# Normalised rows of the expert stage: made on chip from the residual rows, or read from a copy in DRAM

## The chip, the cores and the metric

The kernel runs on one core of a Trainium2 chip. The metric is the device time of one execution in microseconds (us); of several executions the median is given. TensorE (PE) multiplies, VectorE (DVE) and ScalarE (ACT) work on rows, GpSimd (POOL) issues the gathers by index, SyncE (SP) issues all other transfers, and 16 DMA engines carry them out. Each engine takes its instructions in order and waits on semaphores.

## The reference

One layer of a decoder for 1024 prompt tokens and 64 sample tokens (8 sequences of 8, each with 4096 cached positions). What this case is about is the end of the layer:

```
h = x + einsum('btd,de->bte', mixed, w_out)
y = h + peer(rmsnorm(h, norm2_w))
def rmsnorm(x, w):  y = x * rsqrt(mean(x*x, axis=-1) + 1e-6);  return y * w
def peer(xn):       # 8 heads; 128 x 128 product keys
    q = xn @ peer_w_q;  s = q . peer_keys            # two halves of 128 scores a head
    expert = the 16 best pairs of each head;  gate = softmax of their scores
    a = gelu(xn . peer_u[expert])                    # 128 experts a token
    return sum over experts of gate * a * peer_v[expert]
```

Ahead of it stand a projection with pooling mixer and multi-head latent attention (causal over the prompt, paged over the cache for the samples) and a merge with sigmoid gates. Everything is float32; D = 1024. The normalised rows xn are needed twice: transposed for the queries, and row by row for the dots with peer_u.

## The kernel before, in words

Tokens come in nine tiles: eight of 128 prompt tokens and one of 64 sample tokens. The dense work up to the expert scores (class Prompt) is done in three groups of 2, 3 and 3 tiles. Group 0 runs alone; then the expert stage (class Experts) begins and the rest is woven into it: groups 1 and 2, the paged attention of the samples (class Pages), and the dense work of the sample tile (class Sample).

The weaving is by slots. Each engine has a program of the expert stage that yields after each slot (`SLOTS` = 1088 + 20), and `Main.to(slot)` runs that program up to a slot before the dense work emits its next instruction. So the order on every engine is fixed in the code; the slot of a dense piece comes from the class Plan, with planned microseconds.

A slot k belongs to one gather of peer_u and one of peer_v: GpSimd gathers 128 rows of 4 KB by index into a ring of eight buffers (`gather`, L1559), VectorE multiplies them with the normalised rows and sums (`dot`, L1667), after 16 dots come the gelu and a matrix of diagonals, and TensorE multiplies these with the peer_v rows, 20 slots (`LAG`) later (L1622). The buffer of a dot is free for the next gather when the dot is done; that of a peer_v row when its matmuls are.

One gather serves 32 tokens with four heads each, one expert per head, so a dot needs the same 32 normalised rows in each quarter of the 128 partitions: `xrep[j]` holds rows 32j to 32j+31 of the tile four times. There are five such buffers. Their path before the change:

- In the dense part of each group ScalarE squares and sums a row of h (L1152) and takes the root (L1154); VectorE inverts it and multiplies row, inverse and norm weight into `xn2` (L1366, L1368). TensorE transposes `xn2` for the queries (L952).
- SP stores h to `h_dram` (L624) and `xn2` to `xn2_dram` (L626; the trace writes xn_dram). The norm weight, repeated over 128 partitions (512 KB), is loaded in each group (L615) and for the samples (L2172).
- For tile 0 SP loads the four `xrep` buffers with 16 transfers (L637). For each later tile SP loads the rows from `xn2_dram` into one buffer `xt` at slot 80 of the tile before (L1588), and ScalarE copies them into `xrep[j]` in `replicate`, four copies of 32 rows for each j (L1636), 24, 12, 8 and 4 slots before the tile begins; the copies wait until the old content of the buffer has been used.
- The residual rows are loaded from `h_dram` at slot 60 of their tile (L1593), VectorE adds the experts' sum to them (`collect`, L1708), and SP stores the output (L1604).

SP's order around the first group: rows are stored as they come (`keep_rows`), the first three query weights are loaded (`load_peer`, L640), SP waits for the stores, issues the 16 loads, then the loads of the next group (`begin`), then the fourth query weight and the scores' stores (`keep_scores`).

Of the kernel before, what the change touches and what calls it, by code (L numbers as in the profile page):

```python
# [8 lines left out]
ALU = mybir.AluOpType  # L9
# [5 lines left out]
P = 128  # L15
# [64 lines left out]
def build(nc, I, O):  # L80
    with ExitStack() as ctx:
# [7 lines left out]
        for name, shape in (("new_rows", [NS, KL + DR]), ("s_dram", [ROUTES, P, 2 * NK]), ("h_dram", [TOK, D]), ("xn2_dram", [TOK, D]),  # L89
# [197 lines left out]
class Prompt:  # L287
# [145 lines left out]
    def norm2(self):  # L433
        return self.buf(18496, D)

# [43 lines left out]
    def begin(self, main, g):  # L479
# [7 lines left out]
        else:  # L487
            sp.wait_ge(self.rows_stored, 32 * g.tile0)
# [8 lines left out]
        if g.first:  # L497
# [3 lines left out]
            sp.dma_start(self.wukT[0:DN], I["w_ukT"]).then_inc(self.ukT_in, 16)  # L501

# [86 lines left out]
    def load_merge(self, main, g):  # L589
# [25 lines left out]
        sp.dma_start(self.norm2(), I["norm2"]).then_inc(self.res_in, 16)  # L615

    def keep_rows(self, main, g):
        env = self.env
        for t in range(g.tiles):
# [5 lines left out]
            sp.wait_ge(self.xn2_done, tile + 1)  # L625
            sp.dma_start(env["xn2_dram"][dst, :], self.xn2(t)).then_inc(self.rows_stored, 16)  # L626
# [6 lines left out]
        sp.wait_ge(self.rows_stored, 32 * (g.tile0 + g.tiles))  # L633
# [513 lines left out]
    def act_out(self, main, g):  # L1147
        s, ps, st = self.nc.scalar, self.ps, self.stats()
        for q in range(g.tiles):
# [4 lines left out]
            s.activation(st[:, 12 + q:13 + q], st[:, 8 + q:9 + q], ACT.Sqrt, bias=self.C["eps"], scale=1.0 / D).then_inc(self.root2_done, 1)  # L1154
# [198 lines left out]
    def dve_out(self, main, g):  # L1353
        v, ps, st = self.nc.vector, self.ps, self.stats()
        for q in range(g.tiles):
            dve, tile = main.to(g.after("out7", q)), g.tile0 + q
            dve.wait_ge(self.h_done, tile + 1)
            if q == 0:
                dve.wait_ge(self.res_in, 16 * (g.tile0 + g.tiles + g.i + 1))
            y = self.x_row(q)  # L1360
            v.tensor_tensor(y, y, ps[:, 2 + 2 * q:4 + 2 * q, :].rearrange("p a b -> p (a b)"), ALU.add).then_inc(self.h_out, 1)
        for q in range(g.tiles):
            dve, tile = main.to(g.at(f"tp{q}")), g.tile0 + q
            dve.wait_ge(self.root2_done, tile + 1)
            r = st[:, 12 + q:13 + q]
            v.reciprocal(r, r)  # L1366
            v.drain()
            v.scalar_tensor_tensor(out=self.xn2(q), in0=self.x_row(q), scalar=r, in1=self.norm2(), op0=ALU.mult, op1=ALU.mult).then_inc(self.xn2_done, 1)  # L1368

    def dve_scores(self, main, g):  # L1370
        v, ps, i = self.nc.vector, self.ps, g.i
        for j in range(2 * H):
# [5 lines left out]
            if j == 0:  # L1378
                dve.wait_ge(self.rows_stored, 32 * (g.tile0 + g.tiles))
# [120 lines left out]
class Experts:  # L1500
# [4 lines left out]
    def __init__(self, env, sem, ps, rt):  # L1505
# [13 lines left out]
        self.xt = take(D)  # L1519
# [5 lines left out]
        self.a, self.a2, self.th, self.wt = take(2, 16), take(16), take(16), take(16)  # L1525
# [4 lines left out]
        self.x0_in, self.xt_in, self.x_set, self.h_in = sem("i_x0_in"), sem("i_xt_in"), sem("i_x_set"), [sem(f"i_h_in{b}") for b in range(2)]  # L1530
# [873 lines left out]
```

## Time and profile before

| | |
|---|---|
| three timed runs | 3970.24, 3991.52, 3993.34 us, median 3991.52 |
| the profiled execution | 3977.99 us, of which the span of the trace is 3976.2 us |
| busy of the span | PE 3064.3 us (77%), DVE 2684.1 (68%), POOL 2394.3 (60%), ACT 957.7 (24%) |
| transferred | 1387.34 MB, 349 GB/s over the span |
| mean granted clock of TensorE | 0.864 of full speed |

The 40 slices of the page show the DMA engines busy 0.4 to 0.5 of the time up to about 400 us, which is group 0, and 0.8 or more in every slice after that, while VectorE's share goes from 0.5 to 0.8 and back. Such shares are means over stages of different kind; what a stage waits for has to be read from the waits inside it. A wait is put down to what came last. DMA share and GB/s belong together: the share is the mean over 16 engines.

### The profile page before, as it was taken

The page shows a single profiled execution, that of the slowest core. Times are in us where ns is not written, and L with a number is a line of the kernel's source. Part 1 is how long each engine was busy: PE and PEld are TensorE (multiplying, and loading weights), DVE is VectorE, ACT ScalarE, POOL GpSimd, SP SyncE. Part 2 cuts the span into 40 slices and gives each one's busy share as a digit, 9 for nine tenths or more (in the row PEclk, how much of TensorE's full clock was granted, in tenths as well). Part 3 has the DMA queues.
Part 4 walks back from the last instruction along what each step waited for, and adds up shares of the span by engine and source line. Part 5 has one row for each costly group of instructions (what it writes and reads, how often), then busy time and mean ns, then how long its engine had stood idle before and what let it go on. Part 6 is the DMA issues. An engine that isn't in the chain of part 4 may idle for free.

```text
span 3976.2 us, 44748 instructions
## 1 busy us (share of the span) xinstructions
PE 3064.3 (77%) x13299; PEld 1596.3 (40%) x13299; DVE 2684.1 (68%) x6876; ACT 957.7 (24%) x1893; POOL 2394.3 (60%) x2196
## 2 busy tenths in 40 slices
PE   8896888996787888876688888888888866663345
PEld 5665435443442544333344444444444434230001
DVE  2312987665578866666788888888878875656653
ACT  2200123111023320120245444443454411100000
POOL 0000565765676566675766676676667676677776
PEclk9798988997998889998899999899989976666668
DMA  4445798999999989999999999899989999999999
GB/s 132 101 154 186 265 372 326 412 408 373 379 401 388 339 338 411 403 402 373 376 370 331 360 376 358 319 386 362 369 331 365 363 402 414 379 397 383 379 396 376
DMA packets 432834, 1387.34 MB, mean 349 GB/s; under 512 B 60553, under 2 KB 118890, under 8 KB 428306
## 3 DMA queue, kind: packets, MB, share of 16 engines
q0 software_dynamic: 313344, 1140.99, 74.5%
q1 hardware_dynamic: 119250, 243.49, 17.4%
q8 instruction: 109, 1.79, 0.2%
q14 instruction: 131, 1.07, 0.1%
HBM read 1354.17 MB, written 30.11 MB: 348 GB/s over the span
## 4 chain that ended last, share of the span: by engine, by line
PE 31%; DVE 20%; POOL 16%; DMA 15%; issue 10%; DVEq 3%; ACT 3%; SPq 1%; ACTq 0%; POOLq 0%
POOL arena L1559 16%; DMA arena<-in_peer_v,arena 8%; PE ps L1622 6%; DVE arena L1667 6%; PE ps L1872 6%; DMA arena<-in_w_peer 3%; PE ps L713 2%; PE ps L979 2%; DMA arena<-in_peer_u,arena 2%; PE ps L922 2%; DVE arena L2026 2%; PE ps L944 2%; PE ps L1903 2%; PE ps L879 1%; PE ps L856 1%
## 5 line engine op out<-in xcount | busy, mean ns | idle before, releaser
L1667 DVE CUSTOM_DVE_ANT_0 arena<-arena 128x1024 f32<-128x1024 f32 x1088 | 1319.7, 1223 | 562.2 <-DMA arena<-in_peer_u,arena 534.8
L1559 POOL DMA_INDIRECT arena<-in_peer_v,arena x1088 | 1194.0, 1097 | 798.2 <-PE ps L1622 503.6
L1559 POOL DMA_INDIRECT arena<-in_peer_u,arena x1088 | 1198.8, 1102 | 756.3 <-DVEq L1497 385.8
L1622 PE MATMUL ps<-arena 128*32 128x512 f32 x4352 | 693.6, 726 | 446.7 <-DMA arena<-in_peer_v,arena 441.4
L1872 PE MATMUL ps<-arena 128*128 128x512 f32 x1056 | 537.8, 633 | 11.0 <-ACT arena L1965 7.4
L1622 PEld LDWEIGHTS ps<-arena 128*32 128x32 f32 x4352 | 145.4, 124 | 852.3 <-issue 846.1
L979 PE MATMUL ps<-arena 128*128 128x384 f32 (+1 forms) x768 | 248.3, 477 | 57.9 <-DMA arena<-in_w_peer 57.6
L1965 ACT ACTIVATE arena<-ps 128x512 f32<-128x512 f32 x264 | 157.9, 598 | 431.6 <-PE ps L1872 430.0
L1872 PEld LDWEIGHTS ps<-arena 128*128 128x128 f32 x1056 | 188.5, 199 | 172.1 <-issue 162.6
L922 PE MATMUL ps<-arena 128*128 128x384 f32 (+1 forms) x768 | 233.0, 459 | 1.4 <-ACT arena L1135 1.4
L2026 DVE TENSOR_REDUCE arena<-arena 128x8 f32<-128x512 f32 x264 | 180.5, 684 | 79.1 <-ACT arena L1965 66.9
L1880 PEld LDWEIGHTS ps<-arena 128*128 128x128 f32 x1056 | 165.1, 197 | 136.7 <-issue 134.8
L1903 PE MATMUL ps<-arena 128*64 128x257 f32 x528 | 153.9, 443 | 81.5 <-ACT arena L1985 81.4
L979 PEld LDWEIGHTS ps<-arena 128*128 128x128 f32 x768 | 150.1, 202 | 144.6 <-issue 78.9
L713 PE MATMUL ps<-arena 128*128 128x384 f32 (+1 forms) x528 | 170.9, 483 | 21.3 <-DVE arena L1207 21.3
L922 PEld LDWEIGHTS ps<-arena 128*128 128x128 f32 x768 | 146.7, 193 | 91.1 <-issue 20.1
L1952 ACT ACTIVATE arena<-ps 128x256 f32<-128x256 f32 (+1 forms) x264 | 107.7, 408 | 277.3 <-PE ps L1858 154.4
L1880 PE MATMUL ps<-arena 128*128 128x64 f32 x1056 | 150.5, 266 | 0.0
L1636 ACT ACTIVATE arena<-arena 32x1024 f32<-32x1024 f32 x120 | 126.4, 1053 | 92.0 <-DVE arena L1667 90.7
L713 PEld LDWEIGHTS ps<-arena 128*128 128x128 f32 x528 | 102.4, 196 | 91.2 <-issue 34.9
L1903 PEld LDWEIGHTS ps<-arena 128*64 128x64 f32 x528 | 76.3, 155 | 138.9 <-ACT arena L1985 93.4
L1858 PE MATMUL ps<-const,arena 128*128 128x128 f32 x528 | 112.8, 296 | 21.4 <-ACTq L1955 12.6
(232 smaller groups left out, 3719.0 us busy)
## 6 DMA issues: line engine op xcount, KB each, us to landing
arena<-in_w_merge SPq DMA_DIRECT2D x32, 1536.0 KB, 9.3
arena<-in_w_peer SPq DMA_DIRECT2D x64, 576.0 KB, 7.0
arena<-in_cache SPq DMA_DIRECT2D x256, 144.0 KB
arena<-in_peer_u,arena POOLq DMA_INDIRECT x1088, 8.2
arena<-in_peer_v,arena POOLq DMA_INDIRECT x1088, 8.2
arena<-in_w_front SPq DMA_DIRECT2D x33, 512.0 KB, 6.7
arena<-in_w_out SPq DMA_DIRECT2D x24, 512.0 KB, 8.8
arena<-s_dram SPq DMA_DIRECT2D x68, 128.0 KB
```

The lines of the kernel that those rows point to most:

```text
L713: last = t.matmul(bank, w[:, k, :], xnT[:, k, :], start=k == 0, stop=k == KD - 1)
L922: last = t.matmul(ps[:, 2 + 2 * (d % 2) + a, 0:T], ring[:, a * KD + k, :], xnT[:, k, 0:T], start=k == 0, stop=k == KD - 1)
L979: last = t.matmul(ps[:, 2 + j % 2, 0:T], self.p_ring(j % 3)[:, k, :], xn2T[:, k, :], start=k == 0, stop=k == KD - 1)
L1559: self.nc.gpsimd.indirect_dma_start(out=ring[:, slot, :], out_offset=None, in_=self.I[table], in_offset=bass.IndirectOffsetOnAxis(ap=self. ...
L1622: mm = self.nc.tensor.matmul(self.acc[32 * j:32 * j + 32, n, :], self.diag[:, (q0 + j) // 16 % DIAGS, (q0 + j) % 16, :], self.v_ring[:, (q ...
L1636: last = self.nc.scalar.activation(self.xrep[jg % self.XBUF][32 * i:32 * i + 32, :], self.xt[32 * j:32 * j + 32, :], ACT.Copy)
L1667: self.nc.vector.tensor_tensor_reduce(out=u, in0=u, in1=self.xrep[jg % self.XBUF], scale=1.0, scalar=0.0, op0=ALU.mult, op1=ALU.add, accum ...
L1872: last = t.matmul(self.key, self.cTp[:, j % 2, k * P:(k + 1) * P], self.wuk[:, k, :], start=k == 0, stop=k == 1)
L1880: last = t.matmul(out, self.cTp[:, j % 2, k * P:(k + 1) * P], self.qlat[:, k, b * NS:b * NS + NS], start=j + k == 0, stop=False)
L1903: last = self.nc.tensor.matmul(self.acc_ps[0:NS, 0:KL + 1], self.scs[gi % 2][:, j, :], self.source(j, par)[:, 0:KL + 1], start=j == 0, sto ...
L1965: self.nc.scalar.activation(self.sqp[:, j % 2, :], self.key, ACT.Square).then_inc(self.ksq_done, 1)
L2026: self.nc.vector.tensor_reduce(out=self.ssn[:, j, :], in_=self.sqp[:, j % 2, :].rearrange("p (h d) -> p h d", h=H), axis=AX, op=ALU.add).t ...
```

## The change

The array `xn2_dram` goes, with its stores and loads. The inverses of the roots of all nine tiles are kept on chip (`rinv`, one column a tile), and the repeated norm weight is loaded once, at the beginning, into a buffer `w2` that takes the place of `xt`. For tile 0 the 16 transfers read the `xn2` buffer on chip in place of DRAM, and SP waits for their landing before it begins the loads of the next group. For each later tile SP loads the residual rows at slot 80 of the tile before (those of tile 0 at slot 0) into one of the two buffers `h`, from which the output is also formed; VectorE makes 32 normalised rows in the first quarter of `xrep[j]` in `normalise`, at the slots of the old copies, and ScalarE copies them into the other three quarters. The stages before the experts use `w2` and `rinv` too.

```
@@ class Prompt: begin, keep_rows
-            sp.wait_ge(self.rows_stored, 32 * g.tile0)
+            sp.wait_ge(self.rows_stored, 16 * g.tile0)
+            if g.i == 1:
+                sp.wait_ge(self.ex.x0_in, 256)
...
             sp.dma_start(self.wukT[0:DN], I["w_ukT"]).then_inc(self.ukT_in, 16)
+            sp.dma_start(self.ex.w2, I["norm2"]).then_inc(self.ex.w2_in, 16)
...
-        sp.dma_start(self.norm2(), I["norm2"]).then_inc(self.res_in, 16)
...
             sp.dma_start(env["h_dram"][dst, :], self.x_row(t)).then_inc(self.rows_stored, 16)
-            sp.wait_ge(self.xn2_done, tile + 1)
-            sp.dma_start(env["xn2_dram"][dst, :], self.xn2(t)).then_inc(self.rows_stored, 16)
...
         if g.first:
+            sp.wait_ge(self.xn2_done, 1)
             for j in range(4):
                 for i in range(4):
-                    sp.dma_start(self.ex.xrep[j][32 * i:32 * i + 32, :], env["xn2_dram"][32 * j:32 * j + 32, :]).then_inc(self.ex.x0_in, 16)
+                    sp.dma_start(self.ex.xrep[j][32 * i:32 * i + 32, :], self.xn2(0)[32 * j:32 * j + 32, :]).then_inc(self.ex.x0_in, 16)
@@ class Experts: sync
+            if k == 0:
+                self.load_rows(sp, 0)
             t, r = divmod(k, 128)
             if r == 80 and t < PT:
-                rows = P if t + 1 < PT else NS
-                need(sp, self.x_set, 4 * t)
-                sp.dma_start(self.xt[0:rows], self.env["xn2_dram"][(t + 1) * P:(t + 1) * P + rows, :]).then_inc(self.xt_in, 16)
+                self.load_rows(sp, t + 1)
             t, r = divmod(k - LAG, 128)
-            if 0 <= t <= PT and r == 40:
-                rows = P if t < PT else NS
-                need(sp, self.stored[t % 2], 16 * (t // 2))
-                sp.dma_start(self.h[t % 2][0:rows, :], self.env["h_dram"][t * P:t * P + rows, :]).then_inc(self.h_in[t % 2], 16)
...
+    def load_rows(self, sp, t):
+        rows = P if t < PT else NS
+        need(sp, self.stored[t % 2], 16 * (t // 2))
+        sp.dma_start(self.h[t % 2][0:rows, :], self.env["h_dram"][t * P:t * P + rows, :]).then_inc(self.h_in[t % 2], 16)
@@ class Experts: replicate (ScalarE), normalise (VectorE)
         t, j = divmod(jg, 4)
-        act.wait_ge(self.xt_in, 16 * t)
-        if jg >= self.XBUF:
-            t0, j0 = divmod(jg - self.XBUF, 4)
-            act.wait_ge(self.u_used, 128 * t0 + 112 + 4 * j0 + 4)
-        for i in range(4):
-            last = self.nc.scalar.activation(self.xrep[jg % self.XBUF][32 * i:32 * i + 32, :], self.xt[32 * j:32 * j + 32, :], ACT.Copy)
+        act.wait_ge(self.x_one, jg - 3)
+        x = self.xrep[jg % self.XBUF]
+        for i in range(1, 4):
+            last = self.nc.scalar.activation(x[32 * i:32 * i + 32, :], x[0:32, :], ACT.Copy)
         last.then_inc(self.x_set, 1)
...
+    def normalise(self, dve, jg):
+
+        t, j = divmod(jg, 4)
+        dve.wait_ge(self.h_in[t % 2], 16 * (t // 2 + 1))
+        rows = slice(32 * j, 32 * j + 32)
+        self.nc.vector.drain()
+        self.nc.vector.scalar_tensor_tensor(out=self.xrep[jg % self.XBUF][0:32, :], in0=self.h[t % 2][rows, :], scalar=self.rinv[rows, t:t + 1],
+                                            in1=self.w2[rows, :], op0=ALU.mult, op1=ALU.mult).then_inc(self.x_one, 1)
@@ class Experts: vector, at the end of a slot
+            t = (k + 24) // 128
+            if 1 <= t <= PT:
+                for j, ahead in enumerate((24, 12, 8, 4)):
+                    if k == 128 * t - ahead and j < (4 if t < PT else 2):
+                        self.normalise(dve, 4 * t + j)
```

The class Sample loses its own load of the norm weight and its store of normalised rows in the same way, and the counts of `rows_stored` are halved everywhere.

## Rows read from the trace of the kernel before

**Rows 1.** The dots of the expert stage: ns min/median/max, first and last start.

```profile
L1667 DVE CUSTOM_DVE_ANT_0 arena<-arena x1088: 1206/1224/1294, 416.1 to 3942.9; 128x1024 f32<-128x1024 f32 x182
```

**Rows 2.** Windows: busy us of PE, PEld, DVE, ACT, POOL; clock; DMA; GB/s.

```profile
416.00:1960.00 1544.00, 1255.99 (x5193) 635.23 (x5194) 1068.01 (x2626) 282.58 (x532) 994.58 (x912) 0.89 0.98 376
1960.00:3161.00 1201.00, 1040.61 (x4772) 527.35 (x4772) 1018.88 (x2732) 538.52 (x1043) 811.67 (x736) 0.93 0.96 357
3161.00:3976.00 815.00, 429.49 (x2062) 185.91 (x2060) 480.92 (x1171) 69.84 (x147) 580.27 (x538) 0.71 1.00 391
```

**Rows 3.** Waits, 416 to 1960 us: who waited for whom, us, times, longest.

```profile
DVE arena L1667 <- DMA arena<-in_peer_u,arena: 273.5, 149, 10.5
```

**Rows 4.** Waits of VectorE, 1960 to 3161 us.

```profile
DVE arena L2026 <- ACT arena L1965: 58.9, 52, 3.1
DVE arena L2041 <- ACT arena L1976: 25.8, 16, 3.9
```

**Rows 5.** Waits, 3161 to 3976 us.

```profile
DVE arena L1667 <- DMA arena<-in_peer_u,arena: 261.3, 173, 7.8
```

**Rows 6.** DMA issues, 416 to 1960 us: count, KB each, median us to landing.

```profile
xn_dram<-arena SPq DMA_DIRECT2D x6, 512.0 KB
...
arena<-h_dram SPq DMA_DIRECT2D x4, 512.0 KB, 11.1
...
arena<-xn_dram SPq DMA_DIRECT2D x3, 512.0 KB, 11.5
...
arena<-in_norm SPq DMA_DIRECT2D x2, 512.0 KB, 15.3
```

**Rows 7.** DMA issues, 3161 to 3976 us.

```profile
arena<-h_dram SPq DMA_DIRECT2D x2, 512.0 KB, 9.7
...
arena<-xn_dram SPq DMA_DIRECT2D x1, 512.0 KB, 22.1
...
arena<-in_norm SPq DMA_DIRECT2D x1, 512.0 KB, 9.1
...
xn_dram<-arena SPq DMA_DIRECT2D x1, 256.0 KB
arena<-xn_dram SPq DMA_DIRECT2D x1, 256.0 KB, 8.8
arena<-h_dram SPq DMA_DIRECT2D x1, 256.0 KB, 8.5
```

**Rows 8.** The normalisation of 128 rows in the dense part.

```profile
L1368 DVE SCALAR_TENSOR_TENSOR arena<-arena x8: 1284/1285/1286, 284.2 to 1711.9; 128x1024 f32<-128x1024 f32 x8
```

**Rows 9.** ScalarE's copies, 1960 to 3161 us; no wait stands below them.

```profile
L1636 ACT ACTIVATE arena<-arena x48: 1039/1053/1057, 2058.9 to 2971.4; 32x1024 f32<-32x1024 f32 x48
```

**Rows 10.** Timeline of ScalarE at one site of the copies: start us, us.

```profile
2478.30 4.24 ACT L1636 ACTIVATE arena<-arena 32x1024 f32<-32x1024 f32 x4
```

**Rows 11.** Timeline of VectorE for tile 5's sites, with idle time before.

```profile
2479.87 0.28 DVE L1442 MATCH_REPLACE8 arena<-arena 128x128 f32<-128x128 f32 x1
...
2484.88 0.35 DVE L2041 RECIPROCAL arena<-arena 128x32 f32<-128x32 f32 x1 [3.34 <-ACT arena L1976]
...
2555.97 0.69 DVE L2026 TENSOR_REDUCE arena<-arena 128x8 f32<-128x512 f32 x1 [2.52 <-ACT arena L1965]
```

**Rows 12.** Landing of the normalised rows' loads (L1588).

```profile
DMA to landing us min/median/max: 7.7/10.4/22.1
```

**Rows 13.** The gathers of peer_u on GpSimd: ns min/median/max.

```profile
L1559 POOL DMA_INDIRECT arena<-in_peer_u,arena x1088: 932/938/2455, 369.4 to 3932.4; - x182
```

**Rows 14.** The 16 loads of tile 0, and their landing.

```profile
L637 SPq DMA_DIRECT2D arena<-xn_dram x16: 318/421/427, 295.7 to 302.5; - x16
...
DMA to landing us min/median/max: 2.7/3.7/5.9
```

**Rows 15.** Timeline of SP, 303 to 309 us.

```profile
306.34 1.23 SPq L640 DMA_DIRECT2D arena<-in_w_peer  x2
```

**Rows 16.** Timeline of TensorE, 285 to 330 us.

```profile
318.80 6.55 PE L979 MATMUL ps<-arena 128*128 128x256 f32 x16 [12.78 <-DMA arena<-in_w_peer]
```

More of the change, by code:

```diff
@@ L431, in xn2 @@
         return self.buf(15424 + D * t, D)
-    def norm2(self):
-        return self.buf(18496, D)
     def xn2T(self, g):
@@ L1153, in act_out @@
             s.drain()
-            s.activation(st[:, 12 + q:13 + q], st[:, 8 + q:9 + q], ACT.Sqrt, bias=self.C["eps"], scale=1.0 / D).then_inc(self.root2_done, 1)
+            s.activation(self.ex.rinv[:, tile:tile + 1], st[:, 8 + q:9 + q], ACT.Sqrt, bias=self.C["eps"], scale=1.0 / D).then_inc(self.root2_done, 1)
         for q in range(g.tiles):
@@ L1358, in dve_out @@
             if q == 0:
-                dve.wait_ge(self.res_in, 16 * (g.tile0 + g.tiles + g.i + 1))
+                dve.wait_ge(self.res_in, 16 * (g.tile0 + g.tiles))
+                if g.first:
+                    dve.wait_ge(self.ex.w2_in, 16)
             y = self.x_row(q)
@@ L1364, in dve_out @@
             dve.wait_ge(self.root2_done, tile + 1)
-            r = st[:, 12 + q:13 + q]
+            r = self.ex.rinv[:, tile:tile + 1]
             v.reciprocal(r, r)
             v.drain()
-            v.scalar_tensor_tensor(out=self.xn2(q), in0=self.x_row(q), scalar=r, in1=self.norm2(), op0=ALU.mult, op1=ALU.mult).then_inc(self.xn2_done, 1)
+            v.scalar_tensor_tensor(out=self.xn2(q), in0=self.x_row(q), scalar=r, in1=self.ex.w2, op0=ALU.mult, op1=ALU.mult).then_inc(self.xn2_done, 1)
     def dve_scores(self, main, g):
@@ L1378, in dve_scores @@
             if j == 0:
-                dve.wait_ge(self.rows_stored, 32 * (g.tile0 + g.tiles))
+                dve.wait_ge(self.rows_stored, 16 * (g.tile0 + g.tiles))
             if j % 2 == 0 and (g.i or h >= 2):
@@ L1518, in __init__ @@
         self.xrep = [take(D) for _ in range(self.XBUF)]
-        self.xt = take(D)
+        self.w2 = take(D)
         self.u_ring = take(RING, D)
@@ L1524, in __init__ @@
         self.h = [take(D) for _ in range(2)]
-        self.a, self.a2, self.th, self.wt = take(2, 16), take(16), take(16), take(16)
+        self.a, self.a2, self.th, self.wt, self.rinv = take(2, 16), take(16), take(16), take(16), take(PT + 1)
         self.end = w
@@ L2138, in __init__ @@
         w = over
-        self.wuv, self.x, self.w2, self.xn = take(2, 512), take(D), take(D), take(D)
+        self.wuv, self.x, self.xn = take(2, 512), take(D), take(D)
         self.pring = [take(9, P) for _ in range(2)]
@@ L2294, in vector @@
         dve.wait_ge(self.h_done, 1)
-        dve.wait_ge(self.res_in, 32)
+        dve.wait_ge(self.res_in, 16)
         x = self.x[0:NS]
@@ L2299, in vector @@
         dve.wait_ge(self.std_done, 1)
-        v.reciprocal(self.st[0:NS, 1:2], self.st[0:NS, 1:2])
+        v.reciprocal(self.r, self.r)
         v.drain()
-        v.scalar_tensor_tensor(out=self.xn[0:NS], in0=x, scalar=self.st[0:NS, 1:2], in1=self.w2[0:NS], op0=ALU.mult, op1=ALU.mult).then_inc(self.xn_done, 1)
+        v.scalar_tensor_tensor(out=self.xn[0:NS], in0=x, scalar=self.r, in1=self.w2[0:NS], op0=ALU.mult, op1=ALU.mult).then_inc(self.xn_done, 1)
         for h in range(H):
```

17 lines of the change are left out of this document (7 added, 10 removed).

## The prediction

> **What bounds the kernel now.** The profiled execution was timed at 3977.99 us, 13.5 us under the median 3991.52 of the three timed runs. The expert stage begins with its first dot product at 416.1 us [rows 1] and runs to the end: 1088 slots, each with a gather of 512 KB of peer_u and one of peer_v, a dot on VectorE and a share of TensorE's work. What a slot waits for is the question. I cut the spans and the waits into windows until the answer was one within each, and found three stretches:
>
> - 416 to 1960 us: the DMA engines are busy 0.98 of the time at 376 GB/s [rows 2], and dots wait for peer_u 149 times, 273.5 us in all [rows 3]. Transfers set the pace for most of it.
> - 1960 to 3161 us, where the paged attention of the samples runs beside the experts: VectorE is busy 1018.9 of 1201 us [rows 2]. In the view of waits no row has a dot waiting for a gather; VectorE waits for ScalarE instead, 58.9 and 25.8 us [rows 4]. VectorE and its exchange with ScalarE are the bound; the DMA share of 0.96 is a ring kept full.
> - 3161 to 3976 us: DMA share 1.00 at 391 GB/s [rows 2], dots waiting 261.3 us for peer_u [rows 5]. I take 391 GB/s as the rate at which a byte less pays where transfers bind.
>
> **Bytes that go.** In the first stretch six tiles of normalised rows are stored, three loaded again, four residual tiles loaded, and the norm weight twice: 15 transfers of 512 KB [rows 6]. After the change the residual rows are loaded once, in the slots of the normalised ones (that for tile 0 moves to slot 0, the edge of the stretch): three stay. 12 x 0.524 MB = 6.3 MB, at 391 GB/s 16.1 us. Transfers don't bind all the time there (376 against 391 GB/s), so I take three quarters: **-12 us**, bounds 0 and -16. In the last stretch four transfers of 512 KB and three of 256 KB are concerned [rows 7]; one of each size stays, so 3 x 0.524 + 2 x 0.262 = 2.1 MB go: **-5 us**, all on the path; other bound half of it. In the middle stretch bytes are worth nothing.
>
> **What VectorE gets.** 30 normalisations of 32 rows (four for each of the tiles 1 to 7, two for the samples), 24, 12, 8 and 4 slots ahead of the tile's first dot. The same instruction on 128 x 1024 takes 1.285 us [rows 8]; a row-wise one isn't shortened by having fewer rows, to judge by ScalarE's copy of 32 x 1024 at 1.053 us [rows 9]. With the drain ahead of it, 1.4 us; bounds 1.2 and 1.6, since no row has it with 32 rows. ScalarE makes three copies instead of four, 1.05 us less each time, but now waits for VectorE, which in the middle stretch it never did [rows 9].
>
> Twelve lie in the middle stretch (the 48 copies of [rows 9], four a time). I walked through tile 5's four; the pattern stands three times, one is shown. At 2478.30 us ScalarE begins its four copies [rows 10]; VectorE is in a dot, then in a top-eight search to 2480.15 [rows 11]. The new instruction would follow to about 2481.5, three copies to 2484.7, against 2482.5 for the four: 2.2 us late. VectorE had waited 3.34 us for ScalarE's next root [rows 11], so the 2.2 us pass through. The next two sites come out 2.0 and 0.9 us late in the same way. At the fourth the new instruction fits in front of VectorE's wait of 2.52 us [rows 11] and three copies end where four did: nothing. Mean 1.3 us, x 12 = **+15 us**. Bounds: all absorbed, 0; each at 2.6 us (1.4 on VectorE, then a wait 1.2 longer), 31.
>
> Twelve lie in the first stretch, where VectorE waits for gathers 273.5 us [rows 3]: **+2 us**, bounds 0 and, if that cover is gone just there, 12 x 1.4 = 17. Six lie in the last, under 261.3 us of such waits [rows 5]: nothing.
>
> VectorE's new wait, with every later dot queued behind it, is for the residual rows. They are issued 24 slots (some 75 us, at 3560 us for 1108 slots) before the first use, and the transfer whose slot they take lands in 7.7 to 22.1 us [rows 12]: nobody waits. SP's condition for them is a store issued 50 slots earlier: nothing.
>
> A rule speaks against this part. What the trace shows first: 1088 dots with two operands in SBUF already run beside the gathers [rows 1], and GpSimd's gather has a median of 938 ns against a minimum of 932 [rows 13]. So I give the 30 new instructions no price on GpSimd. The Trainium skill, "SBUF — State Buffer", section "SBUF: two separate sides", says that a VectorE operation with two SBUF inputs and a GpSimd operation that reads SBUF shut each other out for the whole instruction. By that rule the sum would have up to 38 us of held gathers more; by the trace, whose medians disagree with such a price, none.
>
> **The start.** After the first group SP waits for the stores of rows, issues 16 small loads from 295.7 to 302.5 us [rows 14], then the next group's first loads, and at 306.34 us the fourth query weight [rows 15], for which TensorE idles 12.78 us [rows 16]. After the change 1 MB less is in flight, and the first weights no longer wait for a normalised tile. Against it, SP waits until the 16 loads have landed, 2.7 to 5.9 us [rows 14], with five transfers and all score stores queued behind. I put the stores' end 5.5 us earlier (1 MB at the early rate of some 200 GB/s) and the new wait at 3.7, with the issue times as they are, so some 2 us earlier: **-2 us**; bounds -6 (the wait is hidden) and +4 (the stores end no earlier). The norm weight's load moves to the beginning, more than 200 us before its use: nothing. SP's shorter waits for stored rows in later groups are in the bytes. The sample's store and SP's waits there are off the path, since its routes are due long after.
>
> **Sum**: -12 - 5 + 15 + 2 - 2 = -2 us, thus 3976 us for an execution like the profiled one. Three timings of the same program lie between 3970 and 3993; halfway between the profiled execution and the median I add 6.8 and, rounded, predict **3982 us**. Chance 0.5.
>
> **Rivals.**
> 1. *Transfers bind more, VectorE less.* The first stretch gives its 16 us, the last 5, the start 2, the normalisations vanish in waits: -23, or 3955, shifted 3962 us. For it: shares 0.98 and 1.00; against: no dot waits for a gather in the middle. Chance 0.2.
> 2. *Slower: the normalisations become the new bound.* In the middle stretch each is handed on in full by ScalarE, 12 x 2.2 = 26 us, those of the first cost 12 x 1.4 = 17, and of the bytes there only half, 8, comes back: 26 + 17 - 8 - 5 - 2 = +28, or 4006, shifted 4013 us. It decides from about 1.5 us a piece in the middle stretch. For it: VectorE busy 85% there without its drains [rows 2]; against: at one of four sites the price is nil. Chance 0.2.
> 3. *The start gets worse*, +4 for -2, by SP's wait for the 16 landings: +4, 3982, shifted 3989 us. For it the five transfers queued behind; against, a megabyte less. Chance 0.07.
> 4. *GpSimd is held.* Each new instruction stops the gathers for 1.28 us where they bind, 38 us at most: 4014, shifted 4021 us. Against it stand the medians of [rows 13]. Chance 0.03. This is what the Trainium skill's page "SBUF — State Buffer" would make of it, by the section named above; the trace so far disagrees.
>
> That the change doesn't do what it says the code excludes: no copy of the normalised rows in DRAM is left, and the 16 loads of tile 0 read the chip's own memory.
>
> **How the numbers follow.** My case alone spans 3964 to 4000: half of the way to the bounds, and the spread between executions. Rival 1 takes the low end to 3958, rival 2 the top to 4008; some 2 in 10 stay outside. 1%, 40 us, is about what a measurement here can tell from no change. Only tails reach it: of rival 1 below, 0.03; of rivals 2 and 4 above, 0.04; the same has 0.93.
>
> **What would show it.** After the change: a last stretch still at DMA share 1.00 and about 5 us shorter for the same slots; a middle one about 15 us longer, in which dots still never wait for gathers; 90 copies, each first one behind a new VectorE instruction of about 1.28 us; the fourth weight of the first group issued before 306 us. I am wrong if the middle stretch doesn't grow, if VectorE waits for residual rows, if the weight goes out later, or if the gather's median leaves 0.94 us.

## The result

The changed kernel takes 4000.02 us (median of 22 runs, 3977.78 to 4014.71) against 3983.54 (22 runs, 3970.24 to 3998.92): ratio **1.0035, 95% interval 1.0019 to 1.0050**, some 14 us slower where 2 us faster was forecast. It lies inside the range and within 1%, but its sign is not the forecast's. The profiled execution was timed at 3997.43 us. In two later sets of runs (the last five experiments) every kernel, the one before too, took 3 to 4% longer (before 4155 and 4124 us); ratios are always to the kernel before in the same set.

The page of the kernel after, its heading, busy lines and transfers (before: 1387.34 MB):

```profile
span 3995.6 us, 44730 instructions
...
PE 3094.7 (77%) x13299; PEld 1615.7 (40%) x13299; DVE 2722.8 (68%) x6906; ACT 926.2 (23%) x1863; POOL 2399.2 (60%) x2196
...
DMA packets 430083, 1377.38 MB, mean 345 GB/s; under 512 B 60233, under 2 KB 118570, under 8 KB 425554
```

10 MB are gone, VectorE has 39 us more and ScalarE 31.5 less. The windows of the kernel after, cut at the same dots as [rows 2] (dot 457 and dot 825 start at 1969 and 3188 us; columns as there):

```profile
415.00:1968.00 1553.00, 1284.20 (x5193) 649.73 (x5193) 1083.75 (x2636) 270.32 (x519) 994.49 (x911) 0.88 0.96 370
1968.00:3189.00 1221.00, 1038.10 (x4784) 528.93 (x4783) 1036.45 (x2756) 526.12 (x1034) 819.32 (x738) 0.94 0.94 351
3189.00:3996.00 807.00, 434.17 (x2051) 190.80 (x2049) 486.08 (x1168) 62.88 (x139) 577.55 (x536) 0.68 1.00 391
```

In the first stretch fewer bytes are moved, and yet it is longer (1553 for 1544 us) and the DMA share fell from 0.98 to 0.96: the room was not used. A second execution of the same kernel (e4 below) took there what the kernel before took, with 0.97; that is no shorter either. The middle one grew by 17 us between the same dots. The new instructions and the copies behind them (one line: durations min/median/max, first and last start; and who waited):

```profile
L1663 DVE SCALAR_TENSOR_TENSOR arena<-arena x30: 1271/1273/1283, 763.5 to 3768.5; 32x1024 f32<-32x1024 f32 x30
...
  ACT arena L1635: 261.0, 30
...
L1635 ACT ACTIVATE arena<-arena x90: 1053/1054/1061, 764.8 to 3771.9; 32x1024 f32<-32x1024 f32 x90
```

Each of the 30 is waited for by ScalarE, 8.7 us on average and 261 us in all. That isn't all new: in the kernel before, the copies waited for dots at 12 of the sites, since the buffer had to be free. The view of its dots (L1667) has among those who waited for them:

```profile
  ACT arena L1636: 90.7, 12
```

So 170 us of ScalarE's waiting are new. In the first stretch (waits, 415 to 1968 us) the gathers' wait for TensorE was 270.8 us for 256.1 (in the second execution 259.5, 415 to 1960 us, so the rise is hardly more than the two differ by), while the dots' wait for gathers, which I had taken for cover, stayed about what it was [rows 3]:

```profile
POOL arena L1559 <- PE ps L1623: 270.8, 81, 15.8
DVE arena L1675 <- DMA arena<-in_peer_u,arena: 259.9, 150, 10.3
...
ACT arena L1635 <- DVE arena L1663: 125.7, 12, 20.4
```

The waits of the kernel before, same stretch, had in place of the first and the last:

```profile
POOL arena L1559 <- PE ps L1622: 256.1, 78, 21.1
ACT arena L1636 <- DVE arena L1667: 44.3, 8, 9.9
```

In the middle stretch (1968 to 3189 us) no dot waits for a gather, as before. VectorE's waits for ScalarE are about those of [rows 4], and ScalarE's new waits for VectorE stand beside them:

```profile
DVE arena L2039 <- ACT arena L1978: 59.4, 52, 3.1
...
ACT arena L1635 <- DVE arena L1663: 31.5, 12, 4.5
DVE arena L2054 <- ACT arena L1989: 28.3, 15, 4.4
```

### The profile page after: what moved, and what is told of

Read it like the earlier page. It is cut to its first block, busy times and chain, and to the rows that moved or that the text cites. A ratio compares the mean times of both kernels' runs of the same rounds, so it can differ in the third digit from the quotient of the medians.

```text
span 3995.6 us, 44730 instructions
## 1 busy us (share of the span) xinstructions
PE 3094.7 (77%) x13299; PEld 1615.7 (40%) x13299; DVE 2722.8 (68%) x6906; ACT 926.2 (23%) x1863; POOL 2399.2 (60%) x2196
## 4 chain that ended last, share of the span: by engine, by line
PE 31%; DVE 22%; DMA 15%; POOL 15%; issue 9%; DVEq 4%; ACT 2%; ACTq 1%; SPq 1%; POOLq 0%
POOL arena L1559 15%; DMA arena<-in_peer_v,arena 9%; DVE arena L1675 7%; PE ps L1623 6%; PE ps L1885 5%; DMA arena<-in_w_peer 3%; PE ps L977 3%; DMA arena<-in_peer_u,arena 2%; DVE arena L2039 2%; PE ps L920 2%; PE ps L942 2%; PE ps L877 1%; PE ps L711 1%; PE ps L854 1%; PE ps L1916 1%
## 5 line engine op out<-in xcount | busy, mean ns | idle before, releaser
L1559 POOL DMA_INDIRECT arena<-in_peer_v,arena x1088 | 1191.7, 1095 | 813.1 <-PE ps L1623 522.9
L711 PE MATMUL ps<-arena 128*128 128x384 f32 (+1 forms) x528 | 172.5, 485 | 20.4 <-DVE arena L1205 20.4
L1635 ACT ACTIVATE arena<-arena 32x1024 f32<-32x1024 f32 x90 | 94.9, 1055 | 261.7 <-DVE arena L1663 261.0
```

The lines of the kernel that those rows point to most:

```text
L711: last = t.matmul(bank, w[:, k, :], xnT[:, k, :], start=k == 0, stop=k == KD - 1)
L1559: self.nc.gpsimd.indirect_dma_start(out=ring[:, slot, :], out_offset=None, in_=self.I[table], in_offset=bass.IndirectOffsetOnAxis(ap=self. ...
```

## The experiments

The table has the times between the starts of dots 0, 457, 825 and 1087 in each profiled execution, us, and in its last column the time from dot 192 to dot 288, a part of the first stretch in which tile 2's four sites lie (slots 232 to 252). Two executions of the same changed kernel differ by 10 and 16 us in the outer stretches and by 0.6 in the middle one, so the outer columns don't tell small differences. That the middle one does rests on this one pair. The ratios are timed.

| kernel | first | middle | last | dots 192 to 288 |
|---|---|---|---|---|
| before | 1545.0 | 1201.8 | 780.0 | 315.9 |
| after | 1554.3 | 1218.9 | 771.9 | 336.4 |
| after, again | 1544.8 | 1218.3 | 788.2 | 328.2 |
| bytes only | 1530.1 | 1202.0 | 785.0 | 318.0 |
| vector only | 1567.8 | 1215.7 | 785.8 | 337.7 |
| work only | 1557.3 | 1185.8 | 792.0 | 325.3 |
| wait only | 1567.5 | 1217.7 | 783.6 | 333.2 |
| one a tile | 1526.8 | 1195.8 | 782.8 | 316.1 |
| after, lagged | 1540.4 | 1181.1 | 776.7 | 323.6 |
| before, lagged | 1552.7 | 1176.4 | 780.7 | 316.8 |
| one a tile, lagged | 1526.6 | 1174.8 | 785.8 | 317.1 |
| first site early | 1556.3 | 1210.6 | 784.3 | 337.1 |
| lag in first (later set) | 1599.7 | 1304.9 | 813.7 | 338.7 |
| lag in middle (later set) | 1610.6 | 1250.6 | 817.3 | 346.2 |
| wait in first (later set) | 1585.3 | 1252.7 | 807.6 | 343.4 |
| wait in middle (later set) | 1590.6 | 1261.6 | 816.9 | 337.4 |
| three copies (later set) | 1579.2 | 1252.3 | 807.6 | 333.0 |

The five rows of the later sets compare with each other alone. There the middle stretch is some 50 to 100 us longer than the kernel before has it in the table, and from dot 825 to dot 1087 the transfers run at 373 to 381 GB/s for 387 to 395, so a stretch needn't price a wait there as it does in the earlier sets.

**Theories.** For e1 and e2, A: the bytes pay as forecast, some 20 us, and VectorE's part is dear everywhere. B: the saved bytes are worth little, and VectorE's part costs about what the middle stretch shows. When these had decided for A, two more divided VectorE's part. V: its 30 instructions cost. W: what costs is that ScalarE is held until VectorE comes to the site.

### Bytes alone, VectorE alone, and the change again

e1, from the kernel after: the normalisations are left out, and ScalarE copies the rows of h, not normalised, four times.

```diff
-        act.wait_ge(self.x_one, jg - 3)
...
-        for i in range(1, 4):
-            last = self.nc.scalar.activation(x[32 * i:32 * i + 32, :], x[0:32, :], ACT.Copy)
+        act.wait_ge(self.h_in[t % 2], 16 * (t // 2 + 1))
... (and for u_used, as before)
+        for i in range(4):
+            last = self.nc.scalar.activation(self.xrep[jg % self.XBUF][32 * i:32 * i + 32, :], self.h[t % 2][32 * j:32 * j + 32, :], ACT.Copy)
... (and VectorE's normalise is never called)
```

> The changed kernel with its 30 VectorE normalisations left out: ScalarE copies the residual rows four times, un-normalised (that part of the computation is left out), with the old wait for the buffer. It has every byte that the change saves and none of VectorE's work. Theory A (bytes pay as forecast, the added VectorE work is what ate them): about 20 us faster than the kernel before (ratio 0.995), the stretch of dots 0 to 480 some 10 to 12 us shorter than before. Theory B (the saved bytes are worth little because the DMA engines aren't the bound in the first stretch): within 5 us of before. The changed kernel stands at ratio 1.0035.

Measured: 3962.25 against 3986.42 us, **0.9940 [0.9918, 0.9961]**: 24 us gained (16 to 33). The start of the change is in it too.

e2, from the kernel before: VectorE makes the first quarter from xt at the sites of the change, ScalarE waits for it and makes three copies. No byte is saved.

```diff
+        self.nc.vector.drain()
+        self.nc.vector.scalar_tensor_tensor(out=self.xrep[jg % self.XBUF][0:32, :], in0=self.xt[rows, :], scalar=1.0,
+                                            in1=self.xt[rows, :], op0=ALU.mult, op1=ALU.max).then_inc(self.x_one, 1)
...
+        act.wait_ge(self.x_one, jg - 3)
...
-        for i in range(4):
...
+        for i in range(1, 4):
+            last = self.nc.scalar.activation(x[32 * i:32 * i + 32, :], x[0:32, :], ACT.Copy)
```

> The kernel before with all its transfers, but VectorE makes the first quarter of each replicated buffer (one instruction of 32 x 1024 with two operands, 30 times, where the change has its normalisation) and ScalarE waits for it and makes the other three. Theory A (VectorE's work is dear everywhere): 30 to 40 us slower than before (ratio 1.008 to 1.010), since the changed kernel has this and gets 20 back. Theory B (bytes worth little, VectorE's work costs about what the page stretch shows): 15 to 20 us slower (ratio 1.004 to 1.005).

Measured: 4025.47 us, **1.0099 [1.0074, 1.0124]**: 39 us lost (29 to 49). e4 is the changed kernel once more beside them.

> The changed kernel itself beside the others: ratio 1.0035 again, and a second trace of it, to see which of the jumps between the two first traces repeat. Both theories expect the jumps at the tiles' ends (dots 480 to 512, 608 to 640, 736 to 768) again; theory A expects the 8 us lost between dots 64 and 96, which hold no normalisation, to be chance.

Measured: 3995.65 us, **1.0023 [1.0007, 1.0039]**. The halves add up: -24 + 39 = +15, the result's +14. Both came out as A said: the bytes pay in full, and VectorE's part costs twice what B gave it. e2 has its loss in the middle (+14) and in the first stretch, where its one trace shows +23.

### The work or the wait

e5 is e2 without ScalarE's wait: VectorE makes the first quarter, ScalarE makes its three copies from xt without waiting for it (SP waits for VectorE as well before it loads xt again). e6 is the kernel before with a bare drain instruction of VectorE that signals, ScalarE waiting for the signal, and four copies.

```diff
 e5
-        for i in range(4):
+        for i in range(1, 4):
...
+        (first_quarter as in e2, at the same slots)
 e6
+        act.wait_ge(self.x_one, jg - 3)
...
+        self.nc.vector.drain().then_inc(self.x_one, 1)
```

> The kernel before with VectorE's 30 instructions (first quarter of each buffer, as in e2_vector_only, which was 39 us slower than before), but ScalarE makes its three copies from the loaded rows and doesn't wait for VectorE. Theory V (VectorE's time is what costs): 30 to 39 us slower, ratio 1.008 to 1.010. Theory W (what costs is that ScalarE, in whose queue the dense groups' copies stand, is held until VectorE reaches the site): 8 to 15 us slower, ratio 1.002 to 1.004, from the page stretch, where VectorE is the bound.

> The kernel before with its four copies at every site and no work added on VectorE; only ScalarE waits until VectorE has come to the site (a drain there gives the signal). Theory W: 20 to 30 us slower, ratio 1.005 to 1.0075, with the loss between dots 232 and 288 as in e2_vector_only. Theory V: at most 8 us slower, ratio under 1.002, and no loss there.

Measured: e5 3982.93 against 3985.24 us, **0.9994 [0.9981, 1.0007]**; e6 4020.62, **1.0092 [1.0066, 1.0118]**. The wait, with nothing added to either engine but the drain, costs what all of e2 does. The drain isn't priced by itself, but e5 has the same 30 drains. V falls, and W stands, though both sizes were missed: e6 was expected at 1.005 to 1.0075, and e5 at 1.002 to 1.004 by W. The waits of e6 over the whole span, with ScalarE's new one and the gathers' wait for TensorE, which was 503.6 us before:

```profile
POOL arena L1559 <- PE ps L1622: 548.5, 171, 21.7
...
ACT arena L1637 <- DVEq L1661: 223.8, 27, 25.0
```

and those of e5, where it is 496.1:

```profile
POOL arena L1559 <- PE ps L1623: 496.1, 174, 21.1
```

e5 mixes two edits, 30 instructions more on VectorE and one copy of four less on ScalarE. e15 takes them apart: the kernel before with the first copy left out at 29 of the 30 sites (that quarter keeps old rows) and nothing else.

```diff
-        for i in range(4):
+        for i in range(0 if jg < self.XBUF else 1, 4):
```

> The kernel before with ScalarE's first copy of each four left out (29 of the 30 sites; the first quarter of the buffer keeps old rows), nothing on VectorE and no new wait. It prices the copy that the change takes from ScalarE, which the work-only kernel (0.9994) contains together with VectorE's 30 instructions. If work on VectorE is free and the copy is worth nothing: 0.9995 to 1.0005. If the copy taken away is worth as much as the new instruction costs (the page stretch of the work-only kernel was 16 us shorter than before): 0.993 to 0.997, and then VectorE's work alone is +0.003 to +0.006.

Measured: 4106.70 against 4124.27 us, **0.9951 [0.9927, 0.9976]**. So the copy taken away is worth about 20 us (10 to 29), and the 30 instructions with their drains cost about 0.9994/0.9951 = 1.004, 17 us, 0.6 us each (by the two intervals some 6 to 28 us; the two ratios are of different sets). In the change three terms meet: work +17, copy -20, wait +37. They add to +34 where e2 measured +39. The drains are in the first term and in the third.

### Where the wait costs

e13 and e14 are e6 with the wait at the sites of tiles 1 to 3 (first stretch) or 4 to 6 (middle) alone.

```diff
+        if 1 <= t <= 3:              (e14: 4 <= t <= 6, and 12 less)
+            act.wait_ge(self.x_one, jg - 3)
```

> The kernel before with ScalarE's wait on a signal of VectorE at the sites of tiles 1 to 3 alone (the first stretch); nothing else is changed, four copies as before. By the step of the prediction (what is added in the first stretch is covered by VectorE's waits for gathers, +2 us or less) the ratio is 1.000 within 0.001. By the theory that the wait is what costs there too (about 22 us of the first stretch in the traces of the wait-only and vector-only kernels): 1.0045 to 1.006. If all of the wait's price (1.0092 for all 30 sites) belongs to the page stretch: 1.000, and the next run shows 1.009.

> The kernel before with ScalarE's wait on VectorE's signal at the sites of tiles 4 to 6 alone (the page stretch), four copies as before. If the two stretches share the price of the wait as the traces' lengths say (22 us and 16 us of 38): 1.003 to 1.005. If the first stretch hides it: 1.008 to 1.010.

Measured: e13 4124.89 us, **1.0021 [0.9993, 1.0050]**; e14 4142.17 us, **1.0037 [1.0004, 1.0069]**, against 4124.27. The middle's share is about 15 us (2 to 29), as expected if the stretches share the price; that it has all 37 is excluded. For the first stretch the value is 8 us, with an interval of -3 to +20: it lies between the two theories, has room for a price of nothing, and ends just short of the 22 us of e6's trace. The six sites of the last stretch weren't tried alone. Together the two make 23 us of e6's 37.

The kept traces say more than the times here, in the last column of the table. From dot 192 to dot 288 five kernels with neither the wait nor four instructions a tile on VectorE take 315.9 to 318.0 us. The two with the instructions and no wait there take 323.6 and 325.3. The five with the wait take 328.2 to 337.7, e6 with the wait alone 333.2, so 12 to 22 us more than the kernel before. In the later sets it is 343.4 and 346.2 us with the wait against 333.0 to 338.7 without. Around the sites of tiles 1 and 3 nothing of the kind shows: from dot 64 to 160 the changed kernel takes 331.4 us in both executions and e1 330.9, from dot 320 to 416 308.9 and 309.2 against 309.9. So the first stretch pays at tile 2's sites.

### One normalisation a tile

e3b, from the kernel after: VectorE normalises the tile's 128 rows in one instruction, 28 slots ahead, into a buffer xt of their own (three buffers of class Sample move to make room); ScalarE makes four copies with the old waits. The bytes stay saved.

```diff
-        act.wait_ge(self.x_one, jg - 3)
+        act.wait_ge(self.x_one, t)
...
-                    if k == 128 * t - ahead and j < (4 if t < PT else 2):
-                        self.normalise(dve, 4 * t + j)
+            t = (k + 28) // 128
+            if 1 <= t <= PT and k == 128 * t - 28:
+                self.normalise(dve, t)
```

> The changed kernel, but VectorE normalises a whole tile of 128 rows in one instruction of about 1.28 us, 28 slots ahead, into a buffer of its own, and ScalarE makes four copies from it with the old waits (8 instructions in place of 30). It has the bytes of e1_bytes_only (ratio 0.994) and little else. Theories V and W both: ratio 0.9945 to 0.997, 12 to 24 us faster than before and 30 us faster than the changed kernel. If it stays above 0.999, something third is in the change.

Measured: 3967.03 us, **0.9951 [0.9935, 0.9968]**, as expected: 20 us faster than before, some 30 faster than the changed kernel. 8 instructions that nobody waits for at once keep nearly all of what the bytes give (e1: 24).

### Copies six slots later

e7 is the kernel after with the sites at 18, 6 and 2 slots ahead of the tile and 2 behind its start, for 24, 12, 8 and 4; only ScalarE's copies move, so they come when the normalisation is long done. e8 does the same to the kernel before, e9 to e3b.

```diff
-            t = (k + 24) // 128
-            if 1 <= t <= PT:
-                for j, ahead in enumerate((24, 12, 8, 4)):
+            for t in range(1, PT + 1):
+                for j, ahead in enumerate((18, 6, 2, -2)):
```

> The changed kernel with all its VectorE work where it was, but ScalarE's copies six slots later (18, 6, 2 slots ahead of the tile and 2 behind its start, each still ahead of its first dot), so that ScalarE finds VectorE's instruction done. Theory W: 15 to 25 us faster than the changed kernel, ratio 0.997 to 0.999. Theory V: no better than it, ratio 1.001 to 1.0035.

> The kernel before with nothing changed but ScalarE's four copies six slots later, as in e7_lagged_copies (ratio 0.9916). Theory W says that a hold of ScalarE is what costs, and the kernel before has some of it too: its copies wait 90.7 us for dots. If that is worth something, 5 to 15 us faster than before (ratio 0.996 to 0.999), from the places where the wait stood and the page stretch. If e7's lead of 33 us comes from the bytes (24 us) and the saved fourth copy alone, this one stays within 0.1% of before.

> e3b_one_per_tile (ratio 0.9951) with the copies six slots later. If the wait for dots matters there as well: 0.991 to 0.993, equal to e7_lagged_copies or a little better, since VectorE has 22 instructions less; but ScalarE has 30 copies more. If the three-copy form is what makes e7 fast in the page stretch (a stop of 3.2 instead of 4.2 us at each site), this one stays at 0.994 to 0.996.

Measured: e7 3952.77 us, **0.9916 [0.9895, 0.9938]**; e8 3961.53 us, **0.9929 [0.9901, 0.9956]**; e9 3940.77 us, **0.9880 [0.9852, 0.9908]**, the best version, 48 us under the kernel before. All three gained more than was expected (0.997 to 0.999 for e7 by W, 0.996 to 0.999 for e8, 0.991 to 0.993 for e9). The waits of e7 over the whole span (the normalisation was waited for 30 times, 261 us):

```profile
ACT arena L1635 <- DVE arena L1662: 68.0, 5, 26.8
DVE arena L2038 <- ACT arena L1977: 44.8, 50, 2.5
DVE arena L2053 <- ACT arena L1988: 13.6, 14, 2.3
```

But e8 shows that the lag pays 28 us without any normalisation too, nearly all in the middle stretch (1201.8 to 1176.4). There the old place of the copies was itself costly. The waits of e8 in its middle stretch, 1971 to 3147 us, against 58.9 and 25.8 in [rows 4]:

```profile
DVE arena L2025 <- ACT arena L1964: 42.5, 45, 2.5
DVE arena L2040 <- ACT arena L1975: 13.9, 13, 3.8
```

VectorE waits 28 us less for ScalarE, and the stretch is 25 us shorter. So e7 doesn't prove by itself that the new wait was the cost; e6 does. It shows how to be rid of most of it. And the fair partner of a lagged kernel is e8: against that one the change with its lag (e7) is only some 5 us faster, and one normalisation a tile with the lag (e9) some 20. In the outer stretches e8 holds ScalarE less too, 9.9 us in each for 44.3 and 46.4, and neither got shorter (1552.7 and 780.7 us), so a wait of ScalarE isn't dear wherever it stands.

### Is the first site the one? Which stretch does the lag help?

e10, from the kernel after: VectorE normalises the first 32 rows at 40 slots ahead for 24, with the buffer free at that time; the rest stands. e11 and e12 lag the copies of the kernel after for tiles 1 to 3 or 4 to 6 alone.

```diff
 e10
-            t = (k + 24) // 128
+            t = (k + 40) // 128
...
-                for j, ahead in enumerate((24, 12, 8, 4)):
+                for j, ahead in enumerate((40, 12, 8, 4)):
...
 e11 (e12: in (4, 5, 6))
...
+                for j, ahead in enumerate((18, 6, 2, -2) if t in (1, 2, 3) else (24, 12, 8, 4)):
```

> The changed kernel with one of each tile's four normalisations, the first, made 40 slots ahead instead of 24, so that ScalarE's first copies find it done; the other three sites stay. The first site had no wait for VectorE's dots before the change (its buffer is long free), the others had one that ended at most a slot earlier. If the hold at the first site carries the loss: ratio 0.996 to 0.999. If all sites carry it alike: 1.000 to 1.002.

> The changed kernel with ScalarE's copies six slots later for tiles 1 to 3 only, whose sites lie in the first stretch (dense groups 1 and 2 beside the experts). If the hold of ScalarE is what the forecast missed there: the stretch to dot 457 is 10 to 20 us shorter than the changed kernel's 1545 to 1554 us, the middle one as long as its 1218 us, ratio 0.997 to 1.000. If the first stretch's loss is VectorE's work alone: no shorter, ratio 1.002 to 1.0035.

> The same for tiles 4 to 6 only, whose sites lie in the page stretch. The middle stretch should fall from 1218 to about 1181 us as in e7_lagged_copies, the first stay at 1545 to 1554: ratio 0.992 to 0.995. Together with e11_lag_first it should add up to e7_lagged_copies (0.9916) less what tiles 7 and 8 give.

Measured: e10 3996.13 against 3985.73 us, **1.0016 [0.9999, 1.0034]**, between the 1.0023 and 1.0035 of the kernel after and nothing, as expected if no single site carries it: 1 site of 4 isn't it. Its trace says so too. At tile 2's first site ScalarE stood 20.4 us in the kernel after and not at all here, and the dots 192 to 288 take as long (337.1 us). e11 4173.01 against 4155.38, **1.0035 [1.0005, 1.0065]**: no gain over the kernel after, where W expected 0.997 to 1.000. It is what the other case said: 1.002 to 1.0035, if VectorE's work alone makes the first stretch's loss. e12 4140.53, **0.9951 [0.9920, 0.9982]**, about as expected (0.992 to 0.995). The lag's gain is the middle stretch's, and in the first one moving the copies gives nothing that can be measured.

## Why the prediction was wrong

**The bytes were right.** -17 us forecast and -2 for the start; e1, which has both, measured -24 (16 to 33), rival 1's half of the story. Whether the forecast was too small the interval doesn't tell. In e1's trace 15 of it is in the first stretch (forecast 12), none in the middle, as said. The forecast -5 of the last stretch isn't seen in any trace (771.9 to 792.0 us against 780.0, whatever the kernel) and stays open. DMA share and rate there are those of before, 1.00 and 391.

**The middle stretch was right.** Forecast +15, measured +17 in both traces of the changed kernel. So was the mechanism, at the site that was worked out. At tile 5's four sites ScalarE stood 3.25, 3.15, 0.62 and 2.27 us for VectorE; less the copy saved, it was 2.2, 2.1, -0.4 and 1.2 us late for a forecast 2.2, 2.0, 0.9 and 0. The first two are as worked out, the last two were wrong in opposite directions, and that their sum came out is luck. VectorE's timeline there (its dots begin at 2491.24, and at 2477.31 before):

```profile
2494.26 1.27 DVE L1663 SCALAR_TENSOR_TENSOR arena<-arena 32x1024 f32<-32x1024 f32 x1 [0.19 <-issue]
...
2501.10 0.35 DVE L2054 RECIPROCAL arena<-arena 128x32 f32<-128x32 f32 x1 [4.41 <-ACT arena L1989]
```

and ScalarE's:

```profile
2495.57 3.19 ACT L1635 ACTIVATE arena<-arena 32x1024 f32<-32x1024 f32 x3 [3.25 <-DVE arena L1663]
```

From that dot to the inverse of the root 9.86 us pass, 7.57 before [rows 11]: 2.3 us late for a forecast 2.2. ScalarE had begun its four copies without a wait [rows 10]; now it stands 3.25 us for VectorE and saves one copy of 1.05. VectorE pays the difference in its new instruction of 1.27 us and a wait that is 1.07 us longer (4.41 for 3.34).

**The step that failed: "Twelve lie in the first stretch, where VectorE waits for gathers 273.5 us: +2 us", and with it "six lie in the last ...: nothing".** VectorE's part costs 39 us in all (29 to 49, e2), of which the middle holds 14 to 17; some 22 more are outside it, where 2 were forecast. I priced the instruction on VectorE and covered it with VectorE's waits. The cover is in part real, and it is beside the point. The instruction with its drain costs 0.6 us each (e5 against e15), less than its 1.27, and the copy that ScalarE saves, to which I gave no worth outside the middle, pays that back. What costs is that ScalarE now stops until VectorE has come to the same slot, and everything behind it on ScalarE stops with it: for the middle I asked who waits for ScalarE, for the first stretch I didn't. That the wait and its drain alone cost 1.0092 is shown (e6).

How it looks there, at a site of tile 2 beside dense work. Before, ScalarE:

```profile
1259.00 0.57 ACT L1079 ACTIVATE arena<-ps,const 8x384 f32<-8x384 f32 x1
1259.59 4.25 ACT L1636 ACTIVATE arena<-arena 32x1024 f32<-32x1024 f32 x4
1263.87 1.05 ACT L1085 ACTIVATE arena<-ps,const 128x384 f32<-128x384 f32 x2
```

and TensorE:

```profile
1264.50 1.56 PE L822 MATMUL ps<-arena 128*128 128x384 f32 x4 [2.41 <-ACT arena L1085]
```

After, ScalarE:

```profile
1255.86 0.57 ACT L1077 ACTIVATE arena<-ps,const 8x384 f32<-8x384 f32 x1
1262.14 3.19 ACT L1635 ACTIVATE arena<-arena 32x1024 f32<-32x1024 f32 x3 [5.70 <-DVE arena L1663]
1265.35 1.05 ACT L1083 ACTIVATE arena<-ps,const 128x384 f32<-128x384 f32 x2
```

and TensorE:

```profile
1265.99 2.93 PE L820 MATMUL ps<-arena 128*128 128x384 f32 x4 [7.03 <-ACT arena L1083]
```

From the start of ScalarE's L1077 (L1079 before) to that of L1083 (L1085) 9.5 us pass where 4.9 did, and TensorE's matmul waits 7.03 us for 2.41. Behind that matmul on TensorE stand those of the expert stage, whose end frees the peer_v buffers. The gathers' wait for them goes roughly with the time of the kernel: 435.5 us (e9), 488.5 (e1), 503.6 (before), 522.9 and 501.5 (the two of the changed kernel), 548.5 (e6). The second execution of the changed kernel doesn't fit, and so this chain is what the rows at one site show, not a measured cause of the whole loss.

How the 22 us outside the middle are divided is settled in part. Tile 2's four sites in the first stretch cost 12 to 22 us in the five traces with the wait. The timed e13 gives 8 us (-3 to +20) for the whole first stretch and e11 gained nothing, so the lower end is the likelier. What the last stretch has is open: ScalarE waits 103.7 us at its six sites, for 46.4 at four of them before, and no experiment has them alone.

**The start**: -2 forecast, the first dot starts at 415.1 for 416.1 us. But it starts between 415.8 and 421.4 us in the traces that have the old start and between 415.1 and 419.2 in those that have the new one, so no gain is shown. Both terms were off. SP's issue of the 16 loads on chip:

```profile
291.95 11.75 SPq L635 DMA_DIRECT2D arena<-arena  x16
...
309.02 1.09 SPq L638 DMA_DIRECT2D arena<-in_w_peer  x2
```

They start 3.7 us earlier than those of [rows 14] but take 11.75 us for 7.28, and the fourth weight goes out at 309.02 for 306.34 [rows 15], later, against what I said would show the step right; TensorE idles 13.95 us for 12.78 [rows 16]. I had taken the issue times as unchanged. And a small slip: 3976 and 6.8 make 3983 us, not 3982.

**The rivals.** Rival 1's bytes and rival 2's kind of cost were both true at once; I gave them separate cases, and neither in full is what happened. Rival 2 said "each is handed on in full by ScalarE", and decided from 1.5 us a piece: 17/12 = 1.4 in the middle. It priced the first stretch by VectorE's 1.4 us a piece as well, the same omission. Rival 3 isn't seen: the weight went out later, but no later start of the dots shows.

**Rival 4's mechanism is real, and I read the row wrongly.** The median of the peer_u gathers is as in [rows 13]:

```profile
L1559 POOL DMA_INDIRECT arena<-in_peer_u,arena x1088: 932/938/6592, 368.4 to 3952.4; - x182
```

But a median over all gathers hides what happens to those that begin while VectorE reads two operands. VectorE and GpSimd at a site of tile 4, after:

```profile
2148.70 0.94 POOL L1559 DMA_INDIRECT arena<-in_peer_u,arena  x1 [0.30 <-issue]
2149.13 1.28 DVE L1663 SCALAR_TENSOR_TENSOR arena<-arena 32x1024 f32<-32x1024 f32 x1
2149.94 1.28 POOL L1559 DMA_INDIRECT arena<-in_peer_v,arena  x1 [0.30 <-issue]
```

The first gather begins ahead of the normalisation and takes 0.94 us. The second begins inside it, takes 1.28 us and ends 0.81 us after it.

So it is with the rest. In the kernel before, the 476 gathers that begin while VectorE idles take 0.932 to 0.947 us. Of the 943 that begin during a dot the median is 1.194 us, and 754 of them end 0.80 to 0.845 us after the dot does. Of the 132 that begin during a TENSOR_REDUCE of 128x512, which reads one operand, the median is 0.937 us. In the changed kernel 29 gathers begin during a normalisation; 27 of them are lengthened, 14 us in all (12.9 in the second execution). The Trainium skill's "SBUF — State Buffer", section "SBUF: two separate sides", would have each new instruction hold off a gather that begins in it until it ends. The trace agrees, by the 27 of 29. My size for it, 38 us, was nearly three times too large, and what of the 14 reaches the kernel's time no run shows; it can be a part of the 17 us that the instructions cost. It isn't the main loss, since e6 has none of these instructions and loses 37 us.

## What to carry to other kernels

When work moves to another in-order engine and a third piece of work then waits for it, price the wait by what is queued behind the waiting engine in every stage, not only the work by the idle time of the engine that gets it; a kernel with the wait alone and one with the work alone tell them apart (1.0092 and 0.9994 here). If a producer and its consumer are emitted in the same slot on two engines, move the consumer some slots later, and make the product once and early: both together turned a loss of 14 us into a gain of 48. But before crediting the lag, try it on the kernel before: 28 of these 48 us came without the change. And don't judge a hold by the median over all instructions: sort them by what the other engine does when they begin.

## What the hardware showed beside

- Transfers from the chip's own memory to itself take SP longer to issue than the same ones from DRAM: 16 in 11.75 us, 593 ns median busy, against 7.28 us and 421 ns [rows 14], though they land in 2.4 us for 3.7 (medians). One of the 16 took 2.2 us to issue.
- A GpSimd gather that begins while VectorE works on two operands in SBUF ends 0.80 to 0.845 us after VectorE's instruction does (754 of the 943 that begin in a dot, in the kernel before); one that begins beside an idle VectorE or a reduction of one operand takes 0.94 us. Over the kernel before this lengthens the gathers that begin in dots by 330 us in sum.
- A row-wise VectorE instruction on 32 partitions takes what it takes on 128: 1.273 us against 1.285 [rows 8], as the bound from ScalarE's copies had it.
- 30 of these instructions of 1.27 us, with a drain ahead of each, lengthened the kernel by about 17 us (6 to 28), 0.6 us each, and a copy of 1.05 us less on ScalarE, the least busy of the four (24%), shortened it by 20 (10 to 29), 0.7 us each. Other blocks of ScalarE, which VectorE and TensorE wait for, stand behind these copies in its queue.
